# Delta rule's input projection: the first two tiles multiply x before the norm, whose root is applied to the products in PSUM, and the filling products go

## The reference, cut to what matters

```python
# end of the first block
x = x + g2x * _conv_ffn(hx2, rows, ffn_w_up[l], ffn_conv_w[l], ffn_conv_b[l], ffn_w_down[l])
return _rms_norm(x, final_norm_g)           # x * rsqrt(mean(x*x) + 1e-6) * final_norm_g

# start of the second
h = concatenate([meta, x], axis=1)           # 16 meta tokens ahead of the 256
proj = h @ w_in                              # gated_deltanet: 32 tiles of 128 outputs, and 16 columns b, a
qkv, z, b_raw, a_raw = split(proj, ...)
qkv = silu(causal_dwconv(qkv, conv_w))
g = -exp(a_log) * softplus(a_raw + dt_bias)
o = chunk_gated_delta_rule(l2norm(q), l2norm(k), v, g, sigmoid(b_raw))
```

## Time and profile before

| | us |
|---|---|
| median of 3 executions | 1308.34 |
| lowest, highest | 1307.76, 1308.56 |
| the profiled execution, its own time | 1307.04 |
| its span in the trace | 1305.2 |
| TensorE busy in it | 1281.4 (98%) |
| mean granted clock of TensorE | 0.991 of full speed |

### The profile page before, as it was taken

One profiled execution on the slowest core, in us unless ns is written; L12 is line 12 of the kernel. 1 busy time (PEld: TensorE's weight loads), 2 busy tenths in 40 slices (PEclk: granted clock), 3 DMA queues, 4 the chain that ended last, 5 costly groups with the idle time before them and its releaser, 6 DMA issues.

```text
span 1305.2 us, 27580 instructions
## 1 busy us (share of the span) xinstructions
PE 1281.4 (98%) x9759; PEld 1202.3 (92%) x9759; DVE 715.9 (55%) x1657; ACT 713.1 (55%) x1290; POOL 876.1 (67%) x383
## 2 busy tenths in 40 slices
PE   9999999999999999999999999999999999999996
PEld 3688899999988899998899989999999999999996
DVE  3989852223587762467355345545633766555623
ACT  3656554554666664485233247666655556666743
POOL 0447956588778879754223217888798787888794
PEclk9999999999999999999999889999999999999999
DMA  9985265456546656633222214555566564655562
GB/s 368 402 322 191 82 217 155 129 162 184 177 152 195 184 162 192 194 114 98 65 66 66 65 33 149 185 179 181 154 180 195 173 186 150 190 179 177 157 194 69
DMA packets 66023, 217.76 MB, mean 167 GB/s; under 512 B 9896, under 2 KB 17320, under 8 KB 62608
## 3 DMA queue, kind: packets, MB, share of 16 engines
q1 hardware_dynamic: 65936, 216.56, 51.7%
HBM read 215.48 MB, written 1.05 MB: 166 GB/s over the span
## 4 chain that ended last, share of the span: by engine, by line
issue 39%; POOL 36%; PE 21%; ACT 1%; DVE 1%; POOLq 1%; DMA 0%; ACTq 0%; DVEq 0%; SPq 0%
POOL w_lo L616 36%; PE bank L720 9%; PE bank L1039 5%; PE bank L808 5%; POOL w_lo L623 1%; ACT w_hi L1568 0%; POOLq L613 0%; ACT h L1568 0%; POOLq L615 0%; DMA w_raw<-in_s 0%; PE bank L658 0%; PE bank L852 0%; PE bank L659 0%; PE bank L663 0%; PE bank L1021 0%
## 5 line engine op out<-in xcount | busy, mean ns | idle before, releaser
L616 POOL TENSOR_TENSOR w_lo<-w_raw,w_hi 128x1024 fp32r<-128x1024 f32 x340 | 814.1, 2404 | 387.9 <-ACT w_hi L1568 386.2
L1568 ACT ACTIVATE w_hi<-w_raw 128x1024 fp32r<-128x1024 f32 (+1 forms) x372 | 378.0, 1020 | 130.1 <-PE bank L808 51.1
L720 PE MATMUL bank<-a_hi,w_hi 128*128 128x264 f32 (+3 forms) x704 | 200.5, 285 | 0.1
L720 PE MATMUL bank<-a_hi,w_lo 128*128 128x264 f32 (+3 forms) x704 | 200.2, 284 | 0.0
L720 PE MATMUL bank<-a_lo,w_hi 128*128 128x264 f32 (+3 forms) x704 | 200.0, 284 | 0.0
L697 PE MATMUL bank<-a_parts,w_hi 128*128 128x256 f32 x960 | 173.8, 284 | 0.2
L697 PEld LDWEIGHTS bank<-a_parts,w_hi 128*128 128x128 f32 x960 | 149.7, 192 | 1.0 <-ACTq L1825 0.5
L697 PE MATMUL bank<-a_parts,w_lo 128*128 128x256 f32 x480 | 135.8, 283 | 0.0
L720 PEld LDWEIGHTS bank<-a_hi,w_hi 128*128 128x128 f32 x704 | 132.9, 189 | 0.4 <-DVE a_lo L3452 0.3
L720 PEld LDWEIGHTS bank<-a_lo,w_hi 128*128 128x128 f32 x704 | 132.9, 189 | 0.1
L720 PEld LDWEIGHTS bank<-a_hi,w_lo 128*128 128x128 f32 x704 | 132.9, 189 | 0.0
(11 more groups left out here) (498 smaller groups left out, 3052.5 us busy)
## 6 DMA issues: line engine op xcount, KB each, us to landing
w_raw<-in_s SPq DMA_DIRECT2D x284, 512.0 KB, 3.6
w_raw<-in_down SPq DMA_DIRECT2D x48, 512.0 KB, 3.6
adaw<-in_w_ada SPq DMA_DIRECT2D x16, 1024.0 KB, 10.3
w_raw<-in_down SPq DMA_DIRECT2D x24, 384.0 KB, 3.2
adab<-in_w_ada_first SPq DMA_DIRECT2D x8, 1024.0 KB, 8.8
ctxt<-in_ctx SPq DMA_DIRECT2D x1, 1024.0 KB, 11.8
x<-in_x SPq DMA_DIRECT2D x1, 1024.0 KB, 15.7
out_h<-h SPq DMA_DIRECT2D x4, 256.0 KB, 2.7
```

The costliest lines, as they stand in the source:

```text
L616: pool.tensor_tensor(w_lo[:, s], w_raw[:, s], w_hi[:, s].bitcast(F32), ALU.subtract) \
L720: ins = mm(banks[bank][:, tk], w_[:, s, k], x_[:, k, tk], start=(m == 0), stop=(m == 3 * KD - 1))
L1568: return nc.scalar.activation(out_, in_, f, **kw)
```

## The change

Two new operands, `m_hi` and `m_lo`, hold the two parts of x times the gain of the norm, without the root. ScalarE writes `m_hi` for a feature tile right after it has squared it, inside `down0`. VectorE writes `m_lo` right after the sum of squares. The meta tokens are put into both at tile 6. All operands of these VectorE instructions are in SBUF. The loops of both engines over the 8 tiles are now written out.

TensorE multiplies tiles 0 and 1 of `a_in` with `m_hi` and `m_lo`, one tile after the other. It waits for seven feature tiles of `m_lo` before the first product. The norm's three products stand after the fourth feature tile of tile 0. The mask transposes come after tile 1, and the twelve filling products are gone. Tiles 2 and 3 are now the ones taken together with `ba`, from the normed operand. Then comes tile 4. VectorE multiplies the banks of tiles 0 and 1 with the inverse root, after the normed operand is complete, and `tap3` waits for that.

```diff
@@ -216,6 +216,10 @@
         half_sum = at("half_sum", [P, KD, 2 * N1], area_a)[:, 0:2, 0:N1]
+        m_hi = at("m_hi", [P, KD, N2], area_a + 17536, F32R)
+        m_lo = at("m_lo", [P, KD, N2], arena + 47872, F32R)
         N2W = N2 + 2
         a2_hi = at("a2_hi", [P, KD, N2W], area_a, F32R)
         a2_lo = at("a2_lo", [P, KD, N2W], area_a + 8768, F32R)
@@ -666,12 +670,6 @@
                     if beside is not None:
                         beside(k)
-            def fill(n):
-                for _ in range(n):
-                    mm(banks[3][:, 0:P], ident[:], ident[:], start=True, stop=True)
             def lin(name, n, ops, split=None, its=None, tiles=None, beside=None, together=0, first=0):
                 u0, t0 = UNIT0[name], TILE0[name]
@@ -1185,7 +1183,6 @@
             lin("w_o", N1, half1, S_MERGED)
             up(0, N1, half1, S_F)
             down(0, N1)
-            rms(RMS_END)
             def claim(name):
@@ -1381,14 +1378,40 @@
                 if k == KD - 1:
                     ins.then_inc(stage_done, 1)
+            u0, t0 = UNIT0["a_in"], TILE0["a_in"]
+            for t in range(2):
+                pe.wait_ge(lo_ready, u0 + t + 1)
+                pe.wait_ge(banks_free, t0 + t + 1)
+                for k in range(KD):
+                    if t == 0:
+                        if k == 4:
+                            rms(RMS_END)
+                        pe.wait_ge(split_ready, 8 * S_M + max(k + 1, KD - 1))
+                    for m, (w_, x_) in enumerate(((w_hi, m_hi), (w_hi, m_lo), (w_lo, m_hi))):
+                        ins = mm(banks[t][:, 0:N2], w_[:, t, k], x_[:, k], start=(k == 0 and m == 0), stop=(k == KD - 1 and m == 2))
+                ins.then_inc(unit_used, 1)
             pe.wait_ge(gdn_in, 112)
             for lv in range(1, LOG2P):
                 ins = nc.tensor.transpose(banks[4 if lv <= 4 else 7][:, (lv - 1) % 4 * P:((lv - 1) % 4 + 1) * P],
                                           levels[:, lv], ident[:])
             ins.then_inc(stage_done, 1)
-            fill(12)
-            lin("a_in", N2, whole2, S_H, tiles=(0, 2), beside=ba, together=2)
-            a_in(2, 5)
+            pe.wait_ge(lo_ready, u0 + 4)
+            pe.wait_ge(banks_free, t0 + 4)
+            for k in range(KD):
+                pe.wait_ge(split_hi, 8 * S_H + k + 1)
+                for t in range(2, 4):
+                    mm(banks[t][:, 0:N2], w_hi[:, t, k], a2_hi[:, k, 0:N2], start=(k == 0), stop=False)
+                    mm(banks[t][:, 0:N2], w_lo[:, t, k], a2_hi[:, k, 0:N2], start=False, stop=False)
+                pe.wait_ge(split_ready, 8 * S_H + k + 1)
+                for t in range(2, 4):
+                    ins = mm(banks[t][:, 0:N2], w_hi[:, t, k], a2_lo[:, k, 0:N2], start=False, stop=(k == KD - 1))
+                    if k == KD - 1:
+                        ins.then_inc(unit_used, 1)
+                ba(k)
+            a_in(4, 5)
             pe.wait_ge(rows_ready, 1)
             token_rows(7, (1, 2))
             mm(banks[7][:, 64:64 + HN], ones[0:HN], glsp[:], start=True, stop=True).then_inc(stage_done, 1)
@@ -1927,11 +1950,20 @@
             ffn(0, N1, ACT.Gelu, PV["conv1_w"] + 4 * KF, PV["conv1_b"])
             nc.scalar.preload_act_table(ACT.Sqrt)
-            down(0, square_after("down0"))
+            u0, t0 = UNIT0["down0"], TILE0["down0"]
+            for t in range(KD):
+                for n in range(3 * t, 3 * t + 3):
+                    act.wait_ge(unit_used, u0 + n + 1)
+                    round_unit(u0 + n + 4, n % SLOTS)
+                act.wait_ge(banks_free, t0 + t + 5)
+                fn(sq[:, t, 0:N1], x[:, t], ACT.Square).then_inc(sq_ready, 1)
+                if t == KD - 2:
+                    act.wait_ge(stage_in, 80)
+                    fn(m_hi[:, :, 0:META], h[:, :, 0:META], ACT.Copy)
+                fn(m_hi[:, t, META:], x[:, t], ACT.Copy, scale=column("final_g", t)).then_inc(split_hi, 1)
             root(RMS_END, N1, 0)
             act.wait_ge(gdn_in, 112)
             fn(wba_hi[:], wba[:], ACT.Copy).then_inc(wba_rounded, 1)
-            act.wait_ge(stage_in, 80)
             split(S_H, whole2[0], h, normed, 8)
             u0, t0 = UNIT0["a_in"], TILE0["a_in"]
@@ -1942,6 +1974,8 @@
             def tap3(p):
                 act.wait_ge(unit_used, u0 + p + 1)
+                if p < 2:
+                    act.wait_ge((conv_scaled, val_scaled)[p], 3)
                 if p == 16:
                     act.wait_ge(stage_done, DONE["hq"])
                 w = PV["a_conv"] + 3 * 24 + A_ORDER[p]
@@ -2774,10 +2808,9 @@
             def down(name, take):
                 u0 = UNIT0[name]
-                with dve.Fori(0, 2) as it:
-                    for j in range(4):
-                        dve.wait_ge(unit_used, it * 12 + (u0 + 3 * j + 3))
-                        take(it * 4 + j, j)
+                for t in range(KD):
+                    dve.wait_ge(unit_used, u0 + 3 * t + 3)
+                    take(t, t % SLOTS)
             for k in range(KD):
                 dve.wait_ge(split_hi, 8 * S_O + k + 1)
@@ -2810,6 +2843,11 @@
                     if s < 3:
                         dve.wait_ge(sq_ready, t + (8 * i + 1))
                         add_to_sum(i - RMS_F, t, s, sq[:, ds(t, 1), 0:N1])
+                    dve.wait_ge(split_hi, 8 * S_M + t + 1)
+                    if t == KD - 2:
+                        v.tensor_tensor(m_lo[:, :, 0:META], h[:, :, 0:META], m_hi[:, :, 0:META].bitcast(F32), ALU.subtract)
+                    v.scalar_tensor_tensor(m_lo[:, t, META:], x[:, t], col("final_g", t), m_hi[:, t, META:].bitcast(F32),
+                                           ALU.mult, ALU.subtract).then_inc(split_ready, 1)
                 begin_sum()
                 return take
@@ -2961,7 +2999,12 @@
             down("down0", residual(RMS_END, "down0", 5))
             inverse(RMS_END, N1)
             dve.wait_ge(stage_in, 80)
+            dve.wait_ge(split_ready, 8 * S_M + KD)
             normalise(S_H, hx, N1, whole2, h, None, lambda k: col("final_g", k), x, rstd[:, 0:N1])
+            for t, scaled in enumerate((conv_scaled, val_scaled)):
+                dve.wait_ge(unit_used, UNIT0["a_in"] + t + 1)
+                tile = banks[t][:, META:N2]
+                v.tensor_tensor(tile, tile, rstd[:, 0:N1], ALU.mult).then_inc(scaled, 1)
             def causal(w, shift, first, n=N2):
                 return (w, lambda ap: ap[:, first:n], lambda ap: ap[:, first - shift:n - shift])
```

More of the change, by code:

```diff
@@ L342, in bass_two_blocks @@
         LN_FROM = (Z0, B1, B2, B3)
-        S_X, S_GU, S_O, S_MERGED, S_N, S_F, S_H, S_ON, S_LN0, S_LN1, S_U, S_LN2 = range(12)
+        S_X, S_GU, S_O, S_MERGED, S_N, S_F, S_M, S_H, S_ON, S_LN0, S_LN1, S_U, S_LN2 = range(13)
         whole = (a_hi, a_lo)
@@ L380, in scaled_before @@
         def scaled_before(i):
-            return 2 * KF * (i - 1) + 2
+            return 2 * KF * (i - 1) + 3
         def normed_in(k):
```

## The result

The changed kernel is slower: 1315.89 us (median of 9 runs, 1312.16 to 1316.75) against 1308.12 us (9 runs, 1306.18 to 1311.95). The ratio is 1.0059, with a 95% interval of 1.0046 to 1.0071. The nine times fall into two groups, three at 1312.2 to 1313.3 and six at 1315.8 to 1316.75. The profiled execution took 1315.89 us, its span is 1313.9 us and its granted clock 0.987. Before, these were 1307.04, 1305.2 and 0.991. So 8.7 us of span have to be found.

What follows compares the result with a forecast made beforehand. TensorE, busy 98% of the span, was taken as the bound. Waits of 4.4 us plus 1.5 for the clock gave 5.9 on 1307.04, so 1312.9, or 1314.2 on the median's scale; range 1309.8 to 1317.2.

Steps and rivals of the forecast that it cites:

- both waits: TensorE idling about 3 us ahead of tile 0 for `m_lo` and 5 to 6 us ahead of tile 4 for `w_lo`.
- The clock: Half-clock stretches after idling ahead of tiles 0 and 4: bounds 0 and 4.5 us, 1.5 taken.
- The wait for `m_lo`: Ahead of tile 0: VectorE's SBUF-only instructions alternate with GpSimd's remainders, so tile 0 starts at 545.2 instead of 542.30, +2.9 us.
- Queued behind it: Behind `m_lo` of tile 6: the addition to x ends at 545.7, hidden by half a microsecond before the norm's products at 546.7.
- The norm is hidden: Ahead of tiles 2 and 3: the first low part is ready at 552.2, the transposes end at 553.2, 1.0 us of cover.
- The last `ba` product: At the end of tiles 2 and 3: starts at 562.1 with the `m_lo` wait, 559.2 at best.
- The remainder of tile 4: Ahead of tile 4: ends 5.8 us after the last `ba` product starts, with 5.8 us of idling; tile 4 at 568.0.
- one more slow stretch: After the new idling: 3.4 us more at half clock, costing 1.5 us, taken as likeliest.
- the rival with three or more slow stretches: Rival (e), the clock falls three times or more: +4.4 + 4.5 and more, 1317.2 and up; chance 0.07.
- the likeliest one, with none to two: Rival (a), both waits as forecast with none to two more slow stretches: 1312.7 up to 1315.7; chance 0.68.
- the median's scale: Whole kernel: the median shown was 1.3 above the profiled execution, so 1312.9 became 1314.2.
- Delay taken up later: Rival (d), in the delta rule: something other than TensorE sets the pace, time within 2 us of 1308.3; chance 0.05.

Runs made afterwards that it cites:

- the two halves: The changed kernel with the meta tokens' low part at tile 6 written by two instructions of 64 elements instead of one of 128: 1317.72 us.
- The first experiment: The changed kernel with ScalarE's rounding of tile 4's weights moved ahead of the work on `ba`, right behind the last high part: 1314.05 us.
- the trace with the filling products: The changed kernel with 22 filling matmuls ahead of tile 0 and 46 ahead of tile 4, in a bank not in use: 1310.84 us.

## Why the prediction was right

The forecast was 1314.2 with a range up to 1317.2, and the median is 1315.9. The direction, both waits and their owners came as foretold. The clock was under-sized, and that the time still lies within the range is in part luck.

- **The wait for `m_lo`.** Forecast: the sum, the meta part and tile 6 each behind one remainder, tile 0 at 545.2. Seen: 2.37, 2.48 and 2.57 us, tile 0 at 545.46. The alternation was argued from the earlier trace rows before, and is now shown by the two halves. The cost at tile 0 is 2.65 us of waiting; the tile starts 3.2 us later than `down0` ended before.
- **The page "SBUF — State Buffer"** of the Trainium skill, section "Who interferes with whom", says that a VectorE instruction with two inputs in SBUF contends with a GpSimd instruction that reads SBUF, and that one with at most one such input, outside the two-port modes, does not. The rows agree again: 2.40 us for 64 elements with two, and 0.47 us for 256 with one in PSUM.
- **Queued behind it.** The addition to x for tile 7 ended at 545.71 (forecast 545.7), and the norm's products did not wait. They started at 548.32 instead of 546.7: 1.4 us because the products ahead of them ran at half clock, and 0.26 by the later start of tile 0.
- **The norm is hidden.** Its first low part ended at 553.69 and TensorE came to it at 554.86, so 1.2 us of cover (forecast 1.0). VectorE made the others faster than they were used.
- **The last `ba` product** started at 563.84 and not at 562.1. The 1.7 us are the half clock at tile 0 (1.4) and the later start of tile 0 (0.26). The price of 0.125 us for a product was a little low for the 72 with `ba`, which took 9.38 us before (0.130 each); in the changed kernel they took 9.1, so it did not matter.
- **The remainder of tile 4.** Forecast: 5.9 us from the last `ba` product to tile 4. Seen: 5.79, of it 5.50 idle. The first experiment shows the cause. It also shows what the prediction did not look for: with this wait removed, the decay is the next bound and gives back only 3.6 us. In the kernel before the decay had 2.5 us of cover (ready at 564.2, used at 566.71), which the prediction did not list.
- **The clock is the term that was mis-sized.** I had bounds of 0 and 4.5 us and took one more slow stretch, 1.5. In the profiled execution it was 9.6 us more at half clock, an estimated 4.3 us, near the upper bound. So it is +8.7 where the sum said 5.9, and the difference of 2.8 us is two more stretches (3.0). I had put the extra stretch into a single sum behind tile 4. In fact the first came directly behind the shorter wait, at 545.4. What happened is thus the rival with three or more slow stretches, which I gave 0.07, and not the likeliest one, with none to two. That rival's time was 1317.2, and this execution took 1315.89, which is also the median, because 1.3 us had been added to every time for the median's scale and this execution did not need them. That is the luck: 1307.04 + 4.4 + 4.5 is 1315.9. The three runs at 1312.2 to 1313.3 had a granted clock of 0.990 to 0.992 against 0.986 or 0.987 of the six others; so they are the ones with less of the slow clock, and near the case that I had forecast.
- **Delay taken up later.** It was not: the 6.0 us at tile 4 were 5.9 at the second group of small products and 8.7 at the end.

What stays open: why the later stretches of slow clock (582 and 753 us) came. TensorE is busy all the time in them, and the trace with the filling products, 20 and 190 us ahead of them, has none there. There is one trace of each kernel, and the kernel before, unchanged, ran at clocks from 0.986 to 0.994 over 52 executions. So where a late stretch falls is not shown to follow from an edit; only that the changed kernel has more of the slow clock over nine executions (0.987 against 0.992) and less again with the filling (0.993). This also bounds what the differences of the medians can say: each holds a few us of late clock beside the place that was edited.

## What to carry to other kernels

Work that is moved to close one gap takes its cover with it. Before moving it, list what was in time only because that work stood there (here the rounding of the next weights, 0.4 us of cover, and the decay, 2.5 us), and which chain sets the end once the cover is gone (here `ba` and its decay). Moving the bulk alone gained nothing even with both waits mended; with that chain's first product moved as well it brought the 4.3 us. An idle time of some 3 us on TensorE can cost more than its length, as the clock may fall behind it: 4.0 us up to tile 4 for a wait of 2.65. It is no fixed multiple, for where only the filling was taken out of a wait of some 3 us the median rose by just 0.85 us, which is not clear of no change. Short VectorE instructions with two SBUF operands that stand back to back each cost one whole instruction of a busy GpSimd, so count them, not their elements.

## What the runs showed that I had not expected

- How strictly VectorE and GpSimd take turns: 64 elements took 2.40 and 2.37 us, 128 took 2.48 and 256 took 2.57, each within 0.2 us of the remainder that GpSimd made beside it (2.38 and 2.46 us, four in 9.53 and 9.82), also when they came back to back. The low part of tile 7, which met only the end of a remainder, took 1.23.
- The price of the clock was about that of the waits it followed: 4.3 us beside 4.4 in the profiled execution. With 68 filling matmuls that compute nothing needed, the changed kernel gained 5.1 us.
- How long the slow clock lasted behind an idle time differed. Behind 3.17 us of idling that ended in small products it was 9.9 us (0.50), of which the last 5 hold tile 5's full products. Behind 5.50 us that ended in full products it was 3.4 us in the changed kernel, and more than that with the meta part one tile earlier (0.50 from 564.4 to 567.8, and 0.59 over the next 3.4 us). The sixteen products of 8 rows took 3.76 us in it and 2.03 at full clock. Whether the small products made it longer is not shown.
